# Layer and RMS norms by token tile in their own banks, one chain of norms at the border of two blocks, rotary angles made in a feed-forward stage

## The reference, cut to what matters

```python
for l in range(2):                                            # first block
    x = layer_norm(DN_ALPHA * x + hybrid_mixer(x, ...), ln1_g[l], ln1_b[l])
    x = layer_norm(DN_ALPHA * x + conv_gated_ffn(x, ...), ln2_g[l], ln2_b[l])
for l in range(2):                                            # second block
    h = rmsnorm(x, norm_mix[l])
    x = x + merged(h) @ w_out[l]
    h = rmsnorm(x, norm_ffn[l])
    gt, up = jnp.split(h @ w_ffn_in[l], 2, axis=-1)
    x = x + (silu(gt) * up) @ w_ffn_out[l]
return rmsnorm(x, norm_final)
```

## Time and profile before

| what | value |
|---|---|
| median of 3 runs | 2322.86 us |
| the profiled execution's own time | 2316.84 us |
| its span, first to last instruction | 2315.0 us |
| PE matmul busy | 2173.9 us, 94% |
| PE weight load busy | 2008.9 us, 87% |
| POOL busy | 1499.2 us, 65% |
| ACT busy | 1076.2 us, 46% |
| DVE busy | 945.6 us, 41% |
| mean granted TensorE clock | 0.965 |

### The profile page before, as it was taken

How to read it: one execution, slowest core, us unless ns; L and a number is a source line. 1 busy time by engine, 2 the same in 40 slices (tenths; PEclk the granted TensorE clock), 3 DMA queues, 4 the chain that set the end, 5 groups by cost and what they waited for, 6 DMA issues and landing times.

```text
span 2315.0 us, 35984 instructions
## 1 busy us (share of the span) xinstructions
PE 2173.9 (94%) x15336; PEld 2008.9 (87%) x15336; DVE 945.6 (41%) x1484; ACT 1076.2 (46%) x1519; POOL 1499.2 (65%) x632
## 2 busy tenths in 40 slices
PE   8999989999878989989999999999999899999998
PEld 7789978799778979879999899888789789998998
DVE  5352356432476536365112211456364561123112
ACT  4555555555555252245444444472532354544444
POOL 6689877698844233356778788663333567687886
PEclk9999989999988989999999999999999999999999
DMA  8336544355523122234445455432122344354553
GB/s 338 139 129 217 184 136 152 122 185 188 183 92 120 55 73 74 86 127 140 158 161 185 149 186 190 150 128 82 65 92 74 109 146 164 130 185 159 182 184 135
DMA packets 47183, 333.05 MB, mean 144 GB/s; under 512 B 5168, under 2 KB 5552, under 8 KB 7856
## 3 DMA queue, kind: packets, MB, share of 16 engines
q1 hardware_dynamic: 47024, 330.76, 41.4%
HBM read 329.69 MB, written 1.05 MB: 143 GB/s over the span
## 4 chain that ended last, share of the span: by engine, by line
PE 60%; DVE 8%; ACT 3%; issue 2%; POOL 0%; DVEq 0%; ACTq 0%
PE bank L147 14%; PE bank L149 13%; PE bank L148 13%; PE y L147 2%; PE y L149 2%; PE y L148 2%; PE bank L1738 2%; PE bank L1748 1%; DVE conv L1384 1%; PE bank L1747 1%; PE bank L1671 1%; DVE sc L2347 1%; PE bank L1790 1%; PE bank L1793 1%; PE bank L1566 1%
## 5 line engine op out<-in xcount | busy, mean ns | idle before, releaser
L348 POOL TENSOR_TENSOR w_lo<-w_raw,w_hi 128x1024 fp32r<-128x1024 f32 x602 | 1463.6, 2437 | 798.3 <-ACT w_hi L339 798.2
L339 ACT ACTIVATE w_hi<-w_raw 128x1024 fp32r<-128x1024 f32 x602 | 636.4, 1059 | 1038.6 <-PE bank L149 868.2
L147 PE MATMUL bank<-x_hi,w_hi 128*128 128x256 f32 x2960 | 878.7, 297 | 27.8 <-POOL w_lo L348 17.1
L148 PE MATMUL bank<-x_lo,w_hi 128*128 128x256 f32 x2960 | 849.3, 287 | 0.0
L149 PE MATMUL bank<-x_hi,w_lo 128*128 128x256 f32 x2960 | 849.0, 287 | 0.0
L147 PEld LDWEIGHTS bank<-x_hi,w_hi 128*128 128x128 f32 x2960 | 580.0, 196 | 53.2 <-issue 25.5
L148 PEld LDWEIGHTS bank<-x_lo,w_hi 128*128 128x128 f32 x2960 | 580.4, 196 | 10.5 <-issue 8.6
L149 PEld LDWEIGHTS bank<-x_hi,w_lo 128*128 128x128 f32 x2960 | 579.2, 196 | 0.0
L876 DVE SCALAR_TENSOR_TENSOR conv<-bank,par_sb,conv 128x254 f32<-128x254 f32 (+1 forms) x176 | 76.8, 478 | 239.8 <-ACT conv L864 238.3
L1246 DVE TENSOR_TENSOR hid_lo<-hid,hid_hi 128x512 fp32r<-128x512 f32 x22 | 45.1, 2049 | 241.2 <-ACT hid_hi L1241 241.2
L147 PE MATMUL y<-w_hi,hid_hi 128*128 128x512 f32 x352 | 139.9, 397 | 3.3 <-DVE hid_lo L898 3.3
(11 more groups left out here) (397 smaller groups left out, 3250.8 us busy)
## 6 DMA issues: line engine op xcount, KB each, us to landing
w_raw<-w SPq DMA_DIRECT2D x300, 1024.0 KB, 4.8
ln_rows<-ln_rows SPq DMA_DIRECT2D x4, 1024.0 KB, 7.3
mem_tok<-mem SPq DMA_DIRECT2D x2, 1024.0 KB, 7.1
const_sb<-const SPq DMA_DIRECT2D x1, 1536.0 KB, 9.8
par_sb<-par SPq DMA_DIRECT2D x2, 553.5 KB, 10.9
xn<-xT SPq DMA_DIRECT2D x1, 1024.0 KB, 4.9
w_raw<-w SPq DMA_DIRECT2D x2, 512.0 KB, 5.5
x_tok<-x SPq DMA_DIRECT2D x1, 1024.0 KB, 8.5
```

What stands on the lines that cost most here:

```text
L147: pe.matmul(out, lhs[0], rhs[0], start=start, stop=False, skip_group_check=skip)
L148: pe.matmul(out, lhs[0], rhs[1], start=False, stop=False, skip_group_check=skip)
L339: act.activation(self.hi[:, h % HALVES, :], self.raw[:, n % RAWS, i * HW:(i + 1) * HW], ACT.Copy).then_inc(*sig.up("high", h))
L348: pool.tensor_tensor(self.lo[:, h % HALVES, :], self.raw[:, n % RAWS, i * HW:(i + 1) * HW], self.hi[:, h % HALVES, :].bitcast(F32), ALU.su ...
```

## The change

- `by_tokens` now takes a unit and a count. It is applied at every norm: the last two halves before each `Norm1` and `Norm2`, the last four before the border and before the end.
- `Norm1` and `Norm2` give each token tile its own banks, 0 to 3 for tile 0 and 4 to 7 for tile 1, so tile 1 is turned only after `y` was read (`var` or `x_new` of tile 1). ACT does the scaling of tile 0 or of half of it, `x_hi`/`x_lo` are made 128 columns at a time (16 instructions on an engine), the table of roots is loaded ahead, and in `Norm2` the mean square comes from ACT's `Square` with an accumulator. ACT's copy `w_hi` of the half four ahead is now emitted behind the norm.
- A class `Border` replaces the last `Norm1` and the first `Norm2` by one chain; its rows of the layer norm are two fused DVE instructions for 512 columns, with `x_tok` and `ln_rows` as inputs.
- The angles move into `Feed1` of layer 1: nine DVE instructions behind the hook of unit 8 (`up 3`), the two sines on ACT behind unit 14 (`up 5`), two more DVE instructions behind unit 18 (`val 6`). SP's load of the positions stands behind `ln1` of layer 1.
- In `Feed1` of layer 1 `down 8` and `down 9` come after `val 10`.

```diff
-    def by_tokens(self, first):
+    def by_tokens(self, last, count):
+        first = last + 1 - count
+        group = range(first, last + 1)
+        self.parts[2 * first:2 * (last + 1)] = [(h, part) for part in range(2) for h in group]
...
 class Feed1:
-            if i:
+            if 0 < i < (11 if l < DEPTH - 1 else 9):
                 self.units.append(self.add_down(i - 1))
...
+    def sp(self, sp):
+        if self.l == DEPTH - 1:
+            sp.wait_ge(*sig.at("var", "ln1", self.l, 1))
+            sp.dma_start(m["turns"][:, 0, :].bitcast(I32), net.a["positions"].to_broadcast([P, T])
+                         ).then_inc(*sig.up("pos_loaded", by=16))
...
     def act(self, act):
+        if self.l == DEPTH - 1:
+            main.act(act, self.after_unit(14))
+            act.wait_ge(*sig.at("reduced"))
+            act.activation(net.tables[:, 2:4, :], m["angle"][:, :, :], ACT.Sin).then_inc(*sig.up("sined", 0))
+            act.activation(m["half_sine"][:, :, :], m["angle"][:, :, :], ACT.Sin, scale=0.5).then_inc(*sig.up("sined", 1))
+            main.act(act, self.end() - 2 * HALVES)
+        else:
+            main.act(act, self.end() - 4)
     def dve(self, dve):
+        if self.l == DEPTH - 1:
+            main.dve(dve, self.after_unit(8))
+            self.net.angles(dve)
+            main.dve(dve, self.after_unit(18))
+            self.net.cosines(dve)
+        main.dve(dve, self.end())
...
 class Norm1:
+        self.tb = [[net.bank[4 * tt + i] for i in range(4)] for tt in range(TT)]
...
+    def act(self, act):                       # root, features as before, one token tile each
+        main.act(act, self.end() - 4)
+        act.preload_act_table_set("sqrt_and_others")
+        main.act(act, self.end() - 2)
+        root(0)
+        act.wait_ge(*sig.at("inverse", *k_l))
+        act.wait_ge(*sig.at("product", self.after().last))
+        for half in range(2):
+            act.activation(net.xn[:, 0, c], net.xtok[:, 0, c], ACT.Identity, scale=net.rs[:, 0:1], bias=net.sd[:, 0:1]
+                           ).then_inc(*sig.up("xn_act", *k_l, 0, half))
+        root(1)
+        for tt in range(TT):
+            for i in range(4):
+                features(tt, i)
+        main.act(act, self.end())
+    def dve(self, dve):
+        net.main.dve(dve, self.end())
+        statistics(0, 0)
+        statistics(0, 1)
+        variance(0)
+        statistics(1, 0)
+        inverse(0)
+        dve.scalar_tensor_tensor(net.sd[:, 0:1], net.mv[:, 0, 0:1], -1.0, net.rs[:, 0:1], ALU.mult, ALU.mult
+                                 ).then_inc(*sig.up("inverse", *k_l))
+        statistics(1, 1)
+        variance(1)
+        inverse(1)
+        for half in range(2):
+            dve.tensor_scalar(net.xn[:, 1, c], net.xtok[:, 1, c], net.mv[:, 1, 0:1], net.rs[:, 1:2], ALU.subtract, ALU.mult
+                              ).then_inc(*sig.up("xn", *k_l, 1, half))
+        for tt, i in TILES:
+            low(tt, i)                        # one tensor_copy, one tensor_tensor, 2x128 columns
...
+TILES = [(0, 0), (0, 1), (1, 0), (0, 2), (1, 1), (0, 3), (1, 2), (1, 3)]
...
 class Norm2:
+    def act(self, act):                       # root: two Squares with accumulator, one Sqrt
+        main.act(act, self.end() - 4)
+        act.preload_act_table_set("sqrt_and_others")
+        root(0)
+        act.wait_ge(*sig.at("inverse", *k_l))
+        act.activation(net.xn2[:, 0, HALF:D], net.xtok[:, 0, HALF:D], ACT.Copy, scale=net.rs[:, 0:1]
+                       ).then_inc(*sig.up("xn_act", *k_l, 0, 1))
+        main.act(act, self.end() - 2)
+        root(1)
+        for tt in range(TT):
+            for i in range(4):
+                high_part(net, act, k_l, self.tb, self.gain, tt, i)
+        main.act(act, self.end())
+    def dve(self, dve):
+        residual(0, 0)
+        residual(0, 1)
+        inverse(0).then_inc(*sig.up("inverse", *k_l))
+        dve.wait_ge(*sig.at("inverse", *k_l))
+        scaled(0, 0)
+        residual(1, 0)
+        residual(1, 1)
+        step(inverse(1))
+        scaled(1, 0)
+        scaled(1, 1)
+        for tt, i in TILES:
+            low_part(net, dve, k_l, self.tb, self.gain, tt, i)
...
+class Border:
+    def act(self, act):
+        main.act(act, self.end() - 6)
+        act.preload_act_table_set("sqrt_and_others")
+        root_first(0)
+        main.act(act, self.end() - 2)
+        squares(0)
+        root(0)
+        root_first(1)
+        act.wait_ge(*sig.at("inverse", *self.second))
+        for half in range(2):
+            act.activation(net.xn[:, 0, c], net.xtok[:, 0, c], ACT.Copy, scale=net.rs[:, 0:1]
+                           ).then_inc(*sig.up("xn_act", *self.second, 0, half))
+        act.wait_ge(*sig.at("par2_loaded"))
+        for i in range(2):
+            high_part(net, act, self.second, self.tb, self.gain, 0, i)
+        squares(1)
+        root(1)
+        for tt, i in ((0, 2), (0, 3), (1, 0), (1, 1), (1, 2), (1, 3)):
+            high_part(net, act, self.second, self.tb, self.gain, tt, i)
+        main.act(act, self.end())
+    def dve(self, dve):
+        def normed(tt):
+            for half in range(2):
+                ins = dve.scalar_tensor_tensor(net.xtok[:, tt, c], net.xtok[:, tt, c], net.mv[:, tt, 0:1], rows[:, 0, c],
+                                               ALU.subtract, ALU.mult)
+            step(ins)
+            dve.wait_ge(*sig.at("root", *self.first, tt))
+            step(dve.reciprocal(net.rs[:, tt:tt + 1], net.sd[:, tt:tt + 1]))
+            for half in range(2):
+                dve.scalar_tensor_tensor(net.xtok[:, tt, c], net.xtok[:, tt, c], net.rs[:, tt:tt + 1], rows[:, 1, c],
+                                         ALU.mult, ALU.add).then_inc(*sig.up("x_new", *self.second, tt, half))
...
+        statistics(0, 0)
+        statistics(0, 1)
+        variance(0)
+        normed(0)
+        statistics(1, 0)
+        square(0)
+        statistics(1, 1)
+        variance(1)
+        inverse(0).then_inc(*sig.up("inverse", *self.second))
+        normed(1)
+        square(1)
+        step(inverse(1))
+        for half in range(2):
+            dve.tensor_scalar(net.xn[:, 1, c], net.xtok[:, 1, c], net.rs[:, 1:2], None, ALU.mult
+                              ).then_inc(*sig.up("xn", *self.second, 1, half))
+        for tt, i in TILES:
+            low_part(net, dve, self.second, self.tb, self.gain, tt, i)
...
 class Mixer2:
     def sp(self, sp):
-        if l == 0:
-            sp.wait_ge(*sig.at("x_final", 3))
-            sp.dma_start(m["turns"][:, 0, :].bitcast(I32), net.a["positions"].to_broadcast([P, T])
-                         ).then_inc(*sig.up("pos_loaded", by=16))
...
     def act(self, act):
-        if l == 0:
-            act.wait_ge(*sig.at("reduced"))
-            act.activation(net.tables[:, 2:4, :], m["angle"][:, :, :], ACT.Sin).then_inc(*sig.up("sined", 0))
-            act.activation(m["half_sine"][:, :, :], m["angle"][:, :, :], ACT.Sin, scale=0.5).then_inc(*sig.up("sined", 1))
...
     def dve(self, dve):
-        if l == 0:
-            self.angles(dve)
```

371 lines of the change are left out of this document (209 added, 162 removed).

## The result

The changed kernel is slower. Eleven runs gave a median of 2327.03 us (2311.84 to 2329.86), eleven of the kernel before 2319.48 us (2316.96 to 2325.93); the ratio is 1.0026, 95% interval 1.0014 to 1.0038. The forecast was 2318 with a range of 2303 to 2327, and faster; the measured time lies just past the upper end, and on the other side of the kernel before. The profiled execution took 2324.56 us with a span of 2322.8 us, 7.8 us more than before; the mean granted clock is 0.965 in both.

What follows compares the result with a forecast made beforehand. PE bounds the kernel, busy 94% of the span, with 82 us of gaps at norms and border. Terms -7.2 + 2 - 3.4 - 5.0 + 8.6 = -5.0 us: 2311.8 against the profiled 2316.84, 2318 against the median 2322.86; range 2303 to 2327.

Steps and rivals of the forecast that it cites:

- RMS norms, -7.2: Three RMS norms: PE starts at E + 6.8 instead of 9.5, first half ends at 10.2 instead of 12.6; -2.4 us each.
- a clock that stays high over the norms: Sign of being wrong: granted clock staying at 2.4 GHz over the norms, which would add 2 us for each.
- Layer norms, +2: Three layer norms: PE starts earlier, but DVE's last pair waits for POOL; first half ends about 15.0, not 14.3; +0.7 each.
- the bound of 16.2: Layer norms: latest end of the first half after E, if last cast and subtraction both wait and the clock is low.
- Border, -3.4: Border: fused instructions go one for one with POOL; PE starts at E + 17.4 instead of 20.5; -3.4 us including `down 10`.
- Angles at the head, -5.0: Head of `Mixer2`: without the angles the 4.78 us stall becomes 0.97, and most of a half-clock stretch goes; -5.0 us.
- Angles in the feed, +8.6: `Feed1` of layer 1: nine DVE instructions delay `hid_lo` of 3, PE idles 5.7 to 8.0 us, plus 1.7 for half clock.
- case A: The forecast itself (0.46): stall in the feed, layer norms even; -12 to +2 us, so 2311 to 2325.
- D: Rival (0.14): slower; all nine angle instructions wait in the feed, PE idles 12.5 to 14.5 us; +1 to +5, up to 2328.
- B: Rival (0.28): the angles are hidden in the feed, costing nothing; -13.6 us in all, 2309.
- C: Rival (0.08): DVE is free of POOL at the border too, and the layer norms' last pair gets through; about 2297.
- E: As rival (0.04): shorter gaps do nothing, ACT ending later, 2323; in times: start of last `y` product plus 0.23 us.

Runs made afterwards that it cites:

- the second pair of profiles: Both kernels, before and after the change, run and profiled again with nothing edited: medians 2318.45 us before, 2324.86 us after.
- pe_filled: The changed kernel with products nobody reads in PE's gaps at every norm and the border: median 2319.32 us, 0.9996 of the kernel before.
- before_filled: The kernel before the change with products nobody reads in PE's gaps at its norms and border: median 2316.80 us, ratio 0.9988.
- angles_late: The changed kernel with the angles' nine DVE instructions one by one behind units 8 to 16, sines behind unit 18: median 2321.08 us.
- w_hi_early: The changed kernel with ACT making `w_hi` right behind the layer norms' first root, before its sixteen `x_hi` instructions: median 2321.62 us.
- held_further: all_four with POOL's `w_lo` held until tile 1's `xn` at the border, its `x_tok` until the layer norms' last `x_lo`: median 2301.52 us.
- after_again: The changed kernel run and profiled once more, nothing edited: median 2324.86 us, 1.0030 of the kernel before.
- pool_behind_norm: The changed kernel, meant to hold POOL's `w_lo` and `x_tok` behind the layer norms' last `x_lo`; only `x_tok` was held: median 2318.58 us.
- angles_at_head: The changed kernel with angles, sines and the positions' load moved back to the start of `Mixer2` of layer 0: median 2340.46 us.
- all_four: The changed kernel with w_hi_early, angles_late, RMS norms' tile 1 squared before `w_hi`, and POOL held through the border's fused rows: median 2303.84 us.
- rms_keys_filled: held_further with unread products in the RMS norms' gaps and at PE's wait for the keys' logarithm in `Mixer2`: median 2298.54 us.

## Why the prediction was wrong

The forecast was -5.0 us; the span grew by 7.8, and by 8.8 in the second pair of profiles. Two steps failed most. At the RMS norms I took an earlier start for an earlier end (off by 6.6 us): the clock and a contended sum took the gain. At the layer norms the mechanism was right and the size too small (off by 7.2). A third term, the stage behind a norm, was put at nothing; it is 6.4 in the first pair and 0.6 in the second. What the `Mixer2` stages gave back, 8.0, was luck for the forecast at least in its larger part.

Each term against the first pair of profiles; a norm is read at its 144th product after E, where the clock has settled, if nothing else is said.

- **RMS norms, -7.2: measured -0.6** (+0.3, -1.2, +0.3). The step "PE starts at E + 6.8 ..., the first half ends at 10.2" failed twice. The start came at 7.4, since "The reciprocal is there at E + 3.4" left out that the sum of two columns, both in SBUF, waits for POOL (1.18 us; the reciprocal came at 4.1). And I ran the 24 products at full clock because they did so after the old gap, though PE's idle time was being moved: they ran at 1.2 GHz, in 5.3 us instead of 3.1. The forecast named a clock that stays high over the norms as a way to be wrong, not one that falls later, just when the products begin. pe_filled and before_filled show that the clock took 1.7 us from the changed and 1.0 us from the old norm. The forecast's 0.27 us for DVE's 128 columns does not follow from the slope it names, which gives 0.31; measured were 0.26, so it cost nothing.
- **Layer norms, +2: measured +9.2** (+4.1, +2.0, +3.1). The mechanism was right: the last pair waits for `w_lo` and for `x_tok`. The size was off. I put the first half's end at 15.0 between 12.0 and 16.2, weighing the case that DVE gets through; both waits came in all three norms, 15.8 to 16.5. A second fall of the clock came behind the new wait, which the bound of 16.2 ("and the clock is low") did not carry on beyond the first half. The last pair itself came at E + 15.0, the 14.9 of the case with both waits. In the second pair of profiles, where the old kernel's clock was high at these norms, the loss is 13.0.
- **Border, -3.4: measured -3.7 at the first product, -2.3 at the end of the first half** (-4.1 in the second pair). PE started at E + 16.9 (forecast 17.4). Two fused instructions in 3.56 and two in 5.26 us are the one for one; alone they took 0.7.
- **Angles at the head, -5.0: measured -5.3** (the gain grows from 2.3 behind the border to 7.6 behind the stall; in the second pair from 4.1 to 6.1, so only 2.0). The stall of 0.96 is the forecast 0.97.
- **Angles in the feed, +8.6: measured +7.9**, of which 7.05 are the angles by angles_late; the other 0.8 was not separated (the new place of `down 8` and `down 9` is one candidate). The block took 17.2 us (forecast 17.9); PE waited 4.51, under the forecast 5.7 to 8.0; half clock behind it came.
- **Not in the sum: +6.4 in `Mixer1` of layer 1** (8.4 less the norm's 2.0), -2.1 and -5.9 in the two `Mixer2`. I ended each norm's account at its first half. Of the 6.4, 5.5 come at the one wait for `aqk` and the half clock behind it. w_hi_early, which lets POOL have its `w_lo` early, is without the wait and brings all of the 8.4 back; but the kernel before has the wait too in one of its two profiles, and held_further lacks it with a late `x_tok`. So what is shown is that a `w_lo` meets the last `aqk` instruction or misses it, not that the norm's delay of `x_tok` is paid there. The -5.9 is no work of the change, as after_again shows (+0.2 for the whole stage in the second pair, the norm included). The -2.1 is -6.1 in the second pair; what makes it is open.

The terms add up to 7.3 us of the span's 7.8. What came was case A's stall with the layer norms' last pair at its upper bound; D's price for that had been put behind a second condition, that all nine angle instructions wait, which did not hold (two of 0.43 and the later ones in 6.32 for three) and was not needed. Rivals B and C, the angles hidden and DVE free of POOL, are excluded by the rows; E by pool_behind_norm and w_hi_early, where the last pair came earlier with ACT's sixteen instructions unchanged. The range was said to begin at B's middle, which is 2309, and began at 2303; it made no difference here.

## What to carry to other kernels

When two engines exclude each other, ask for every short instruction of the critical chain what the other engine runs at that moment, down to a sum of two columns, and move the release of the other's work rather than the chain: one line on ACT took 15.9 us out of three stages, though only 5.4 of the whole by medians, since another stage moved against it. A shorter gap is no gain until you know at which clock the work behind it runs, and an instruction 60 us behind the changed place can meet the other engine or miss it by 0.4 us, which was worth 5.5 us here. Compare stages over more than one profile of the same kernel before you explain a difference, and look inside a stage before you take its length for the effect of an edit: in angles_at_head a loss of 11.1 us at the head showed as 3.7 at the end.

## What the runs showed of the hardware that was not expected

- The smallest instruction waits like a large one: the sum of two single columns took 1.18 us (after) and 1.65 us (all_four) behind a `w_lo`, 0.16 alone. And two scalings with one SBUF input each waited for a `w_lo` each, 4.50 us against 0.88, more than the 2.72 in the earlier trace rows. The rule of the Trainium skill (SBUF — State Buffer, Who interferes with whom) makes no exception for size: for the sum, with its two SBUF inputs, the trace agrees.
- The second fall of the clock after the layer norms' wait: 0.94 at 452 to 454, 0.50 at 456 to 458, with PE idle 2.65 us in between. Held over the gap by products that nobody reads, the clock did not fall at any of the RMS norms (pe_filled, before_filled). But in rms_keys_filled it fell to 1.2 GHz 74 us into `Mixer2` of layer 0 although PE had been busy for the whole of the 8 us before.
- One kernel, same instructions: `Mixer2` of 624.73 and 631.98, of 642.13 and 638.26 us in two profiles, and 2316.7 to 2335.9 us over twelve runs of pool_behind_norm.
